# An attention stage joined to the projection before it, with another planned order

## The reference

```
q      = rmsnorm(q_lat, g_q) @ w_uq             # 8 heads, 128 + 64
q_abs  = einsum('bshn,rhn->bshr', q_nope, w_uk)  # absorbed, 128
ckv    = rmsnorm(kv_lat, g_kv);  kr = rope(k_r, pos)
s      = (q_abs . ckv + rope(q_r) . kr) * 192 ** -0.5, masked causally
o_lat  = softmax(s) @ ckv
```

## Time and profile before

| | |
|---|---|
| median of three runs | 2160.0 us (2158.34 to 2161.67) |
| profiled execution, device time | 2157.53 us |
| its span, first to last instruction | 2155.3 us |
| mean granted TensorE clock | 0.994 |
| TensorE busy | 2091.7 us, 97% |
| VectorE busy | 1298.6 us, 60% |
| ScalarE busy | 973.3 us, 45% |
| GpSimd busy | 356.3 us, 17% |

### The profile page before, as it was taken

The page is one execution under the profiler, slowest core; times in us unless marked ns, Lnnn a source line. Parts: engine busy times, 40 slices in busy tenths (PEclk is TensorE's granted clock), DMA queues, the critical chain, the costliest instruction groups (busy, mean ns, idle before and its releaser), DMA issues.

```text
span 2155.3 us, 31505 instructions
## 1 busy us (share of the span) xinstructions
PE 2091.7 (97%) x11893; PEld 1953.5 (91%) x11893; DVE 1298.6 (60%) x2753; ACT 973.3 (45%) x1729; POOL 356.3 (17%) x499
## 2 busy tenths in 40 slices
PE   7998799999999999999999999999999999999997
PEld 6998688888888887799999999999999999999997
DVE  7775787888878777556444644446444654446434
ACT  4445565655555555554334433344333533344333
POOL 3444121111111101061002300041001400041000
PEclk9999999999999999999999999999999999999999
DMA  8876221111010022354534453434534454334532
GB/s 304 254 229 175 73 53 49 40 31 35 25 30 26 25 103 90 135 169 132 179 99 157 130 180 118 144 115 129 180 116 141 134 173 129 124 112 127 180 117 72
DMA packets 159557, 260.45 MB, mean 121 GB/s; under 512 B 21322, under 2 KB 109778, under 8 KB 158246
## 3 DMA queue, kind: packets, MB, share of 16 engines
q1 hardware_dynamic: 136574, 229.20, 34.3%
q10 hardware_dynamic: 20528, 16.67, 2.7%
q0 software_dynamic: 2304, 12.58, 1.6%
HBM read 216.97 MB, written 41.66 MB: 120 GB/s over the span
## 4 chain that ended last, share of the span: by engine, by line
PE 56%; DVE 1%; ACT 0%; ACTq 0%; issue 0%; POOLq 0%; POOL 0%; DVEq 0%
PE b_ps L122 55%; PE b_ps L2079 1%; DVE d_y L1967 0%; DVE d_y L1987 0%; ACTq L1772 0%; ACT d_wr L1220 0%; DVE d_y L1969 0%; DVE d_wr L84 0%; ACT d_y L1868 0%; POOLq L1598 0%; ACTq L1598 0%; ACT d_zs L1861 0%; ACT d_zs L1844 0%; DVE d_gate_p L1995 0%; DVE d_pool L84 0%
## 5 line engine op out<-in xcount | busy, mean ns | idle before, releaser
L122 PE MATMUL b_ps<-d_ht,d_wr 128*128 128x412 f32 x3840 | 734.8, 349 | 1.7 <-DVE d_wr L84 1.4
L122 PEld LDWEIGHTS b_ps<-d_ht,d_wr 128*128 128x128 f32 x3840 | 715.8, 188 | 6.0 <-DVE d_wr L84 1.7
L84 DVE TENSOR_TENSOR d_wr<-d_ws,d_wr 128x1024 fp32r<-128x1024 f32 x260 | 322.1, 1239 | 551.7 <-ACT d_wr L1220 551.7
L1220 ACT ACTIVATE d_wr<-d_ws 128x1024 fp32r<-128x1024 f32 x260 | 275.0, 1058 | 601.6 <-PE b_ps L122 590.7
L743 PE MATMUL b_ps<-kt,k_qs 128*128 128x512 f32 (+2 forms) x1520 | 323.9, 370 | 6.6 <-DVE b_top L1065 5.7
L743 PEld LDWEIGHTS b_ps<-kt,k_qs 128*128 128x128 f32 x1520 | 267.5, 190 | 53.0 <-DVE b_top L1065 6.0
L1129 PE MATMUL b_ps<-b_pt,kv 128*128 128x512 f32 x816 | 228.3, 410 | 4.6 <-DVE b_pt L84 4.6
L84 DVE TENSOR_TENSOR b_pt<-b_ps,b_pt 128x512 fp32r<-128x512 f32 x272 | 181.7, 687 | 52.2 <-ACT b_pt L1024 50.0
L1017 ACT ACTIVATE b_p<-b_p,b_bias 128x1024 f32<-128x1024 f32 (+7 forms) x192 | 171.4, 895 | 87.9 <-DVE b_low L1076 83.1
L1024 ACT ACTIVATE b_pt<-b_ps 128x512 fp32r<-128x512 f32 x272 | 156.7, 597 | 114.6 <-PE b_ps L1129 59.7
L122 PE MATMUL b_ps<-d_mrg,d_wr 128*128 128x412 f32 x960 | 189.9, 353 | 0.0
(11 more groups left out here) (210 smaller groups left out, 2068.5 us busy)
## 6 DMA issues: line engine op xcount, KB each, us to landing
d_ws<-in_w SPq DMA_DIRECT2D x260, 512.0 KB, 3.6
out_q<-a_qout SPq DMA_DIRECT2D x32, 384.0 KB, 4.7
d_hf<-out_ht SPq DMA_DIRECT2D x20, 412.0 KB, 3.7
d_olf<-out_olat SPq DMA_DIRECT2D x40, 206.0 KB, 2.9
a_xt<-in_x_t SPq DMA_DIRECT2D x16, 512.0 KB, 5.0
out_ht<-a_hf SPq DMA_DIRECT2D x16, 512.0 KB, 3.7
out_olat<-b_ol ACTq DMA_DIRECT2D x32, 256.0 KB, 3.9
out_y<-d_y SPq DMA_DIRECT2D x5, 1536.0 KB
```

Of the source, the lines that this page charges most:

```text
L84: return e.tensor_tensor(low, source, high.bitcast(f32), ALU.subtract)
L122: mm = pe.matmul(out, stationary(a, k), moving(b, k), start=first and k == 0 and a + b == 0, stop=last and k == depth - 1 and a == 1)
L1220: act.activation(ahead["wr"][k % 2][:, 0, :, :], ahead["ws"][k % 4][:, :, :], ACT.Copy).then_inc(ahead["w_hi"], 1)
```

## The change

- project and attend get one block between them. In project, VectorE, TensorE and GpSimd end with waits for what the barrier ensured; SP stores the last half of the queries in project's last step.
- `READY` is 2: units 2 and 3 get their high and low halves in attend's order.
- The planner: TensorE's queues are S, T, V; VectorE's L, P, I, B, C. GpSimd has a queue of its own (W, the low half). Durations are others, and the times at which queries have been loaded (`loaded`) and the time from a low half to the next load's landing (`landing`) are given. The special case for the last unit goes.
- Rows of one chunk (the small units): C evicts minus the scaled scores and their minimum, so that the minimum is the bias; step B falls away, and E has the scale -1.
- The stores of attended values are issued by SP: store(0) to store(3) behind the loads of units 8 and 9, and then store(u - 6) behind load(u).

```diff
-        block = ctx.enter_context(nc.Block())          # project, attend
-                    if i == LAST_STEP:
-                        break
+            pool.wait_ge(q_ok, len(parts))
+            pool.wait_ge(keep["q_ok"], READY)
-                if i in (NT + 1, NT + 2):
-                    for u in (2 * (i - NT - 1), 2 * (i - NT - 1) + 1):
+                if i == NT + 1:
+                    for u in range(READY):
                         query_high(act, keep, u)
+            dve.wait_ge(q_ok, len(parts))
+            dve.wait_ge(kr_ok, NT)
+            dve.wait_ge(qout_d, sum(part.heads is None for part in parts))
+            pe.wait_ge(qout_a, sum(part.heads is not None for part in parts))
+            pe.wait_ge(qcos_ok, sum(part.heads is None for part in parts))
-READY = 4
+READY = 2
...
-        "PE": [list(turns), [("V", *t[1:]) for t in turns], list(scores)],
+        "PE": [list(scores), list(turns), [("V", *t[1:]) for t in turns]],
         "ACT": [[("H", *t[1:]) for t in turns], [("E", u, h, p) for u, h in heads for p in range(parts(u))],
-                [("O", u) for u in range(units)], [("Q", u) for u in range(units)]],
-        "DVE": [[("L", *t[1:]) for t in turns], [("C", *s[1:]) for s in scores], [("B", u, h) for u, h in heads],
-                [("I", u, h) for u, h in heads], [("P", u, h, p) for u, h in heads for p in range(parts(u))]],
+                [("O", u) for u in range(units)], [("Q", u) for u in range(READY, units)]],
+        "DVE": [[("L", *t[1:]) for t in turns], [("P", u, h, p) for u, h in heads for p in range(parts(u))],
+                [("I", u, h) for u, h in heads], [("B", u, h) for u, h in heads if u >= SMALL], [("C", *s[1:]) for s in scores]],
+        "POOL": [[("W", u) for u in range(READY, units)]],
...
-    lag = {("S", "Q"): 2.6, ("Q", "Q"): 7.0}
+    landing = {("Q", "W"): 4.4}
+    loaded = {2: 1.3, 3: 2.2, 4: 6.3, 5: 9.0, 6: 11.5, 7: 13.5, 8: 19.0, 9: 22.0}
...
-            store_q(sp, io, keep, keep["qout"], len(GROUPS_Q) - 1, 1)
...
-            for u in range(SMALL, units):
+            def store(u):
+
+                i, g = query_tile(u), u % NGRP
+                sp.wait_ge(ol_ok, u + 1)
+                sp.dma_start(io["olat"][:, HG * g:HG * g + HG, i * P:i * P + P],
+                             ol[u % 2][:, :].rearrange("p (h t) -> p h t", h=HG)).then_inc(o_out[u % 2], 16)
+
+            load(SMALL)
+            load(SMALL + 1)
+            for u in range(4):
+                store(u)
+            for u in range(SMALL + 2, units):
                 load(u)
+                store(u - 6)
+            for u in range(units - 6, units):
+                store(u)
...
-                    act.wait_ge(bias_ok, HG * u + h + 1)
+                    negated = chunks(u) == 1
+                    if negated:
+                        act.wait_ge(s_sb, number["S", u, h, 0] + 1)
+                    else:
+                        act.wait_ge(bias_ok, HG * (u - SMALL) + h + 1)
                     act.activation(span, span, ACT.Exp, bias=bias[:, at:at + 1],
-                                   scale=SCALE, accum_out=total[:, at, part:part + 1]).then_inc(exp_ok, 1)
+                                   scale=-1.0 if negated else SCALE, accum_out=total[:, at, part:part + 1]).then_inc(exp_ok, 1)
...
-                    act.wait_ge(ol_ok, u + 1)
-                    act.dma_start(io["olat"][:, HG * g:HG * g + HG, i * P:i * P + P],
-                                  ol[u % 2][:, :].rearrange("p (h t) -> p h t", h=HG)).then_inc(o_out[u % 2], 16)
...
+                    if chunks(u) == 1:
+                        dve.tensor_tensor_reduce(out=out, in0=inp, in1=mask[:, 512 - keys:512], scale=-SCALE,
+                                                 scalar=-3 * NEG, op0=ALU.add, op1=ALU.min,
+                                                 accum_out=bias[:, at:at + 1]).then_inc(s_sb, 1)
+                        continue
```

More of the change, by code:

```diff
@@ L176, in query_parts, with project @@
     return parts
-def project(nc, io, keep):
+def project(nc, io, keep, block):
     with ExitStack() as ctx:
@@ L785, in takes @@
         kind, u = step[:2]
-        if kind == "Q" and u < READY:
-            return 0.0
         if kind == "S":
-            return 5 * max(0.11, 0.058 * key_chunks(tiles(u))[step[3]][1])
+            return 5 * max(0.111, 0.0586 * key_chunks(tiles(u))[step[3]][1])
         if kind == "C":
@@ L792, in takes @@
         if kind == "E":
-            return 0.34 + 0.125 * width(u, step[3], PART)
+            return 0.45 + 0.111 * width(u, step[3], PART)
         if kind == "P":
-            return 0.5 + 0.035 * width(u, step[3], PART)
-        return {"T": 0.45, "V": 0.7, "H": 0.6, "L": 0.69, "O": 0.6, "Q": 1.25, "B": 0.24, "I": 0.35}[kind]
+            return (0.22 + 0.065 * width(u, step[3], PART)) if u < SMALL else (0.45 + 0.045 * width(u, step[3], PART))
+        if kind == "I":
+            return 0.16 * (2 * parts(u) - 1)
+        return {"T": 0.44, "V": 0.7, "H": 0.6, "L": 0.69, "O": 0.6, "Q": 1.25, "B": 0.24, "W": 2.6}[kind]
     def needs(step):
@@ L801, in needs @@
             n = at_s[step[1:]]
-            out = [("Q", u)]
+            out = [("W", u)] if u >= READY else []
             if n >= NS:
@@ L813, in needs @@
         if kind == "E":
-            return [("B", u, at[0])]
+            return [("B", u, at[0])] if u >= SMALL else [("C", u, at[0], 0)]
         if kind == "I":
@@ L823, in needs @@
             if u >= SMALL + 2:
-                out.append(("Q", u - 2))
+                out.append(("W", u - 2))
             return out
+        if kind == "W":
+            return [("Q", u)]
         if kind == "O":
@@ L844, in needs @@
         return [("H", u, *at)]
-    lag = {("S", "Q"): 2.6, ("Q", "Q"): 7.0}
+    landing = {("Q", "W"): 4.4}
+    loaded = {2: 1.3, 3: 2.2, 4: 6.3, 5: 9.0, 6: 11.5, 7: 13.5, 8: 19.0, 9: 22.0}
     done, orders = {}, {e: [] for e in queues}
-    now = {e: 0.0 for e in queues}
+    now = {"PE": 0.0, "ACT": 1.3, "DVE": 0.0, "POOL": 0.0}
     while any(q for e in queues for q in queues[e]):
@@ L851, in attend_orders @@
         ready, later = None, []
-        waiting = queues[engine]
-        if engine == "PE" and waiting[2] and waiting[2][0][1] == units - 1:
-            waiting = waiting[2:] + waiting[:2]
-        for queue in waiting:
+        for queue in queues[engine]:
             if queue:
@@ L859, in attend_orders @@
                     continue
-                at = max((done[x] + (x[0] != "Q" or x[1] >= READY) * lag.get((queue[0][0], x[0]), 0.0) for x in wanted), default=-1.0) + 0.1
-                if queue[0][0] == "Q" and 6 <= queue[0][1] < SMALL:
-                    at = max(at, 4.0 + 2.2 * (queue[0][1] - 5))
+                at = max((done[x] + landing.get((queue[0][0], x[0]), 0.0) for x in wanted), default=-1.0) + 0.1
+                if queue[0][0] == "Q":
+                    at = max(at, loaded.get(queue[0][1], 0.0))
                 if at <= now[engine]:
@@ L875, in attend_orders, with attend @@
     return orders
-def attend(nc, io, keep, early):
+def attend(nc, io, keep, early, block):
     with ExitStack() as ctx:
@@ L940, in weights @@
             return sp_[u % 2 * HG + h][:, first + keys.start:first + keys.stop]
-        block = ctx.enter_context(nc.Block())
         @block.sync
@@ L1007, in _ @@
                 if kind == "Q":
-                    if u >= READY:
-                        before = slot_before(u)
+                    before = slot_before(u)
+                    if before >= 0:
                         act.wait_ge(s_ok, number["S", before, HG - 1, chunks(before) - 1] + 1)
-                        query_high(act, keep, u)
+                    query_high(act, keep, u)
                 elif kind == "E":
@@ L1025, in _ @@
                 elif kind == "O":
-                    i, g = query_tile(u), u % NGRP
                     act.wait_ge(v_ok, last_product(u))
@@ L2199, in build @@
         keep["q_in"] += keep["qw_in"] + keep["qh_in"]
-        project(nc, io, keep)
+        block = ctx.enter_context(ExitStack())
+        both = block.enter_context(nc.Block())
+        project(nc, io, keep, both)
         early = early_decode(nc, ctx)
@@ L2212, in build @@
         early["ps"] = keep["ps"]
-        attend(nc, io, keep, early)
+        attend(nc, io, keep, early, both)
+        block.close()
         ahead = merge_ahead(nc, ctx, keep, early)
```

## The result

| | before | after |
|---|---|---|
| median of four runs | 2159.6 us (2158.34 to 2161.67) | 2127.9 us (2125.74 to 2129.85) |
| profiled execution, its span | 2157.5, 2155.3 us | 2128.3, 2126.5 us |
| attention: first score to end of the last product | 189.1 to 857.3: 668.2 us | 190.6 to 829.3: 638.7 us |

The two profiled executions differ by 29.2 us. The sign and the place were right, the size was not.

A forecast was written before the change was run, and what follows sets the result against it. TensorE, busy for 97% of the span, was taken as the bound. Terms of -7.9 - 5.3 + 2 - 3 = -14.2 us on the median of 2160.0 us gave 2145.8 us, about 2146, range 2133 to 2158.

The forecast's parts named there:

- The ceiling: TensorE's losses in attention: 18.5 us at the front and 12 us in the long rest, at most 30.5 us to gain.
- The long rest: Attention from 260 us on: scores beside the start of a unit's transposes gain a quarter of 12 us, -3 us.
- the ten waits for the low half: From 260 us on, transposes wait for VectorE's low half to free a PSUM slot: 10.7 us, falling to about 8.
- rival (c): Slower: scores wait for evictions queued last on VectorE, 1.4 us at each of 24 large units, 2179 us; chance 0.09.
- The 79% of VectorE: VectorE's busy share in the long rest, given as a sign for late evictions stopping TensorE's scores.
- Scores mixed in front: Small units up to 260 us: scores spread over products fill refill gaps, -5.3 us, bounds 0 and -10.6.
- upper bound of 10.6 us: Front loss besides the border's gap and clock, with transposes and products standing alone from 227.88 us; half was forecast.
- The border: Between the two blocks: removal ends a TensorE gap of 5.7 us and 2.2 us of low clock, -7.9 us.
- Stores from SP: Front: store(0) behind load(9) lands at 217 us and holds ScalarE 1 to 8.4 us; +2 us, bounds 0 and +8.
- O(2): ScalarE's third copy of attended values, expected at 208.6 to 215.7 us, waiting for store(0)'s landing at 217 us.
- Negated rows: Small units' rows of one chunk: 32 B steps leave VectorE and a hop leaves each exponential; 0 us.
- GpSimd's port: Front: each GpSimd low half holds a VectorE pass up to about 1.3 us; bounds 0 and +8, taken as 0.

The follow-up runs named there:

- e8: Changed kernel with SP's last query store moved ahead of the loads of units 4 and 5: 2121.0 us, ratio 0.9834.
- e11: Changed kernel with one planner constraint: from unit 8 on, a unit's first transpose comes after the next unit's last score: 2131.6 us, ratio 0.9873.
- e4: Changed kernel with only VectorE's planner queues in the old order (low half, evictions, bias, inverse, normalising): 2140.8 us, ratio 0.9920.
- e10: Kernel before with only the new order of the planner's queues, on TensorE and VectorE: 2150.3 us, ratio 0.9962.
- e2: Changed kernel with the planner's queues in the old order on TensorE and VectorE, and the old last-unit special case: 2153.6 us, ratio 0.9976.
- e5: Changed kernel with the planner's old durations for scores, exponentials, normalising, inverse and transposes; load times and queue W stay: 2135.2 us, ratio 0.9895.
- e9: Kernel before with only the border of the two blocks removed, with replacement waits and the last query store in project: 2155.2 us, ratio 0.9981.
- e1: Changed kernel with the border of the two blocks put back, nothing else: 2131.3 us, ratio 0.9871.
- e6: Changed kernel with the stores of attended values issued by ScalarE again, each behind its copy: 2126.9 us, ratio 0.9860.
- e12: e8 with the stores of attended values issued by ScalarE as before: 2122.9 us, ratio 0.9834.
- e7: Changed kernel with eviction with maximum and bias step B given back to the rows of one chunk: 2129.3 us, ratio 0.9870.

## Why the forecast was too small

**The ceiling was wrong.** "30.5 us in all, and no order can bring more", but attention is 29.5 us shorter with 6 us still lost in front, and e8's is 35.9 us shorter. The rate of a score, 0.298 us a block, came from the busy time of the group (323.9 us over 1088 blocks). Busy time holds the matmuls at the lower clock and the ends of matmuls before a gap, too. From starts to starts at full clock it is 0.293, 5 us less over all the blocks, and the room was 36 us (668.2 less 632). That the rates added up to the busy time of the window confirmed nothing: both came from the same busy times.

**The long rest: -3 us forecast, about -15 measured.** This is the step that failed. I saw the ten waits for the low half, named the cure ("scores lie beside the start of a unit's transposes, where the 10 waits are"), and then took a quarter of the 12 us because scores are held back "in either order". They are held back alike, and that is no limit: what counts for those waits is whether one is left at the first transpose, and two or three remove most of them (e11: 5 us lost, not 15). Nearly all of the idle time was of this one kind (10.7 of 12.0 us), and all of it went; the last 3 of the 15 us are the busy time that the wrong rates had taken for work.

**Evictions last on VectorE: the rival (c) had the wrong sign.** I priced the lateness of evictions at 33 us of loss. With the old order of VectorE's queues, e4 loses 12.9 us: if evictions go first, normalising comes late, TensorE uses up its scores meanwhile, and comes to its transposes with nothing beside them (in 5 of 22 units by the plan; ten waits for low halves from 260 us on). TensorE waited for evictions hardly at all in the kernel after (1.5 us once). The 79% of VectorE were no sign of a coming wait. They are the share of an engine whose work has slack, and an order that lets evictions wait instead of weights used it here at next to no cost.

**Scores mixed in front: -5.3 forecast.** The stretch from 211 to 260 us is without loss, so nearly the whole upper bound of 10.6 us came. The mechanism was put down to the wrong part, though: I ascribed it to scores first, and the queues alone bring nothing in front (e10), while all the rest of the change with the old queues brings 10 us there, the border's share included (e2). The half that I kept back for wrong durations is real (7.3 us in e5), but the change brings figures that fit.

**The border: -7.9 forecast; 4.1 us measured in the kernel before (e9), 3.4 in the changed one (e1).** The gap did go, as said. I had asked whether TensorE has work until 197.6 us, which it has (eight scores), and not what its first product needs. The high half's wait for the query stores stands in the kernel before, too, and costs nothing there, where the first transposes come at 227.88 us, long after the stores. In the changed kernel transposes begin at 197.54 us, and the wait shows: 3.56 us of gap and the clock at 0.50 behind it. e8 removes it and gains 4 to 7 us. Then the border is worth about what its row says: e1, which has the border and finds its stores landed in the gap, is 10.3 us slower than e8 (8 by the ratios, 9.5 in attention). "Where a stall goes, what is late next" was asked at one engine too few.

**Stores from SP: +2 forecast, nothing measured** (e6: -1.0 us, within the uncertainty). SP's row of issues was counted about right: store(0) was issued at 216.88 us (213.2 forecast). What was wrong is the other side of the race. O(2), expected between 208.6 and 215.7 us, came at 224.90 us, after the landing, and waited only for its product:

```profile
224.90 0.60 ACT L1049 ACTIVATE b_ol<-b_ps 128x512 f32<-128x512 f32 x1 [0.51 <-PE b_ps L1150]
```

The hole before 203.6 us makes it late, and the scores that the new order puts first (the order's part is not measured). In e8, which is earlier here, the wait does come:

```profile
219.95 0.60 ACT L1049 ACTIVATE b_ol<-b_ps 128x512 f32<-128x512 f32 x1 [3.35 <-DMA out_olat<-b_ol]
```

TensorE has scores in hand then: it stands for 0.9 us in all from 204 to 260 us, and without this wait, in e12, the time is the same.

**Negated rows and GpSimd's port: 0 and 0.** e7 agrees for the first. For the second no run takes the low halves away, so it is not shown; but VectorE's passes are held up in the kernel after too:

```profile
240.95 1.32 DVE L1114 TENSOR_SCALAR b_p<-b_p,b_inverse 128x256 f32<-128x256 f32 x1
...
242.98 0.35 DVE L1114 TENSOR_SCALAR b_p<-b_p,b_inverse 128x256 f32<-128x256 f32 x1
```

The first of these two equal passes runs while GpSimd makes low halves (239.46 to 242.1 us), the second after them: 1.0 us more. TensorE did not stand in that stretch. Such a row agrees with the exclusive lock that the Trainium skill describes (SBUF — State Buffer, section "SBUF: two separate sides"). It shows in no wait of TensorE here, which stood for 0.05 us from 211 to 260 us.

**What stays open.** Which of the durations, the load times, the planned low halves and `READY` = 2 brings the front's gain has no run of its own, nor is it known why e2 loses 6 us more behind 260 us than the kernel before. Whether step B's absence is worth the 1.5 us of e7 or nothing cannot be told from these intervals. In the profiled run of the kernel after, the scores began 1.5 us later than in before; e1 began at 189.0 and e6 and e7, with the same projection, at 189.6 us, so I take it for scatter and count nothing on it.

## What to carry to other kernels

In an order written ahead for an engine that is the bound, ask of each place where its pipeline must refill (here three PSUM banks and up to 2 us) whether one independent step is left to lie beside it; two or three removed most of the loss here, and many elsewhere don't help. Give a helper engine first to what makes those refills ready, here the weights, and last to what only makes the bound engine's next filler, as long as fillers are left. When a barrier is taken out, list every wait that the steps behind it will now reach sooner, down to buffers that share memory, and bring the latest of them forward; and take rates from starts of back-to-back instructions, not from busy time, before calling a sum a ceiling.

## What the runs showed of the hardware that was not expected

A gap costs two thirds as much again in the clock behind it, at this place. TensorE ran without a gap from 190.60 to 200.06 us at a granted clock of 1.00; then 3.56 us of idleness were followed by a granted clock of 0.50, the 1.2 GHz level, for 4 us, in which nine matmuls took 4.21 us and not 2.31, and by 0.82 for another 3 us, in which 25 matmuls took 3.51 us and not 3.00. The single refill gaps of 1.6 us (before, 750.93 us) and of 2.0 us (e2, 743.96 us) in the long rest left the clock at 1.00 in the stretches behind them. And an execution's busy time of TensorE is no measure of its work: the same attention, matmul for matmul, counts 640.4 us busy in the kernel before and 631.2 in e8:

```profile
189.11:857.31 668.20, 640.44 (x3506) 542.19 (x3505) 517.16 (x1554) 383.25 (x749) 96.43 (x74) 0.99 0.18 53
```

```profile
188.63:820.90 632.27, 631.22 (x3507) 539.33 (x3506) 498.60 (x1490) 381.14 (x748) 93.91 (x74) 1.00 0.19 56
```
